# Head norms of a hybrid decoder step: squares summed in two column groups, inverse roots from exp and ln

## The chip, the cores and the metric

The kernel runs on one core of a Trainium2 chip. The metric is the device time in microseconds of one execution. The core's engines work side by side, each through its own queue in order: TensorE (PE), VectorE (DVE), ScalarE (ACT), GpSimd (POOL) and SyncE (SP); DMAs are issued from SP's, ACT's and POOL's queues. Engines wait for each other through semaphores.

## The reference, cut to what matters

One inference step of a one-layer decoder on 512 prompt tokens and 8 x 4 sample tokens, 544 tokens in all. Two branches (retention, and gated linear attention, GLA) have four heads each. The output of each head is normalised over its 128 channels, multiplied by a gain and by a gate, and projected; both branches are mixed by sigmoid gates, and a gated ConvFFN follows.

```python
def group_rmsnorm(o, g):
    B, L, H, dv = o.shape
    of = o.astype(jnp.float32)
    y = of * lax.rsqrt(jnp.mean(of * of, axis=-1, keepdims=True) + EPS)
    y = y.reshape(B, L, H * dv) * g.astype(jnp.float32)
    return y.astype(o.dtype)
...
    y_r = (group_rmsnorm(o_r, g_ret) * jax.nn.silu(rg)) @ w_ret_out
...
    y_g = (group_rmsnorm(o_g, g_gla) * jax.nn.silu(gg)) @ w_gla_out
    mix = jax.nn.sigmoid(m_r) * y_r + jax.nn.sigmoid(m_g) * y_g
    h = x + mix @ w_o
```

The model-wide norms (`rmsnorm` with ln1, ln2, and the last one) have the same form over 1024 channels.

## The kernel before, in words

Activations lie transposed: channels on the 128 partitions, the 544 tokens along the free axis, in two halves of 272 (`HALF`), since a PSUM bank takes one half. All large products are made of three single-pass products of a high and a low part of weights and activations (`whi`, `wlo`, `nhi`, `nlo`): ACT copies a weight block from `raw` to `whi`, DVE subtracts to get `wlo`, and SP loads the next block when `wlo` is done.

The stage of the change is the middle of the program. `middle_order()` writes one list of steps, and each engine walks through that list and issues its own part of every step. The order of every queue is thus written by hand. The list goes through 15 units of 256 columns of the input projection (PE: `product`, line 2050; two halves j of 128 columns), and puts the small steps of the branches between them. Steps that matter here, for head h: `gsq`/`rsq` (ACT squares the head's output into `gsq`), `gn`/`rn` (PE sums the squares over the partitions by a matmul with ones; ACT takes the square root), `gi`/`ri` (DVE inverts the root and scales the head), `sl` (ACT's silu of the gate, tile `ysil`), `y1` (DVE: head times gate), `y2` (ACT makes the high part `yhi`, DVE the low part `ylo`), `rk`, `rs`, `rp`, `ro`, `rx`, `rw` (the retention of one head: keys, masked scores, states, output, sample states). g is GLA, r is retention. The eight norms come in the order gn0, gn1, gn2, gn3, rn0, rn1, rn2, rn3.

The small products share PSUM tile `ax`, two banks at a time in turn: PE takes banks (`aux_take`) when the use two before is drained, sets `aux_filled`, and the engine that reads them sets `aux_drained`. The roots go to `grs` and `grs1` in turn, so norm n waits until DVE has scaled norm n-2 (`o_ready`). There is one `gsq` for the head norms: a square waits until PE has summed the one before.

The parts of a head norm, one line for each engine:

```python
run(gsq[:, :], normed(NORMS[n]), ACT.Square, osq_done)                      # ACT, L1160
small(bank(name, a)[:, 0:HALF], ones, sq[:, HALF * a:HALF * (a + 1)], ...)  # PE, L2089
run(halves(grs2[norms % 2][:, :]), bank2(s), ACT.Sqrt, drained_sem(s), scale=1.0 / DV, bias=eps)  # ACT, L1165
inverse(root[:, :], s, dve_step)                                            # DVE, L1648
dve.scalar_tensor_tensor(normed(s), normed(s), vec(...), root[:, :], ...)   # DVE, L1653
```

After the list come the gate units (`GATES`): PE computes the sigmoid gates of the two branches in two units of two halves each, and DVE drains each half from PSUM into `gsig` (line 1465, `scaled`). A second gate unit's half j begins on PE when the first unit's half j is drained:

```python
for j in range(2):
    pe.wait_ge(drained[j], F0[j] + g)
    product(j, u % 2, j, every, nhi, nlo).then_inc(filled[j], 1)
```

DVE reaches that first drain after the last steps of the list, which are `ri` 3, `y2` 5, `y1` 6, `y1` 7, `y2` 6, `y2` 7. POOL begins there to add weight blocks in DRAM by accumulating DMAs (`v_weight_sum`).

Of the kernel before, what the change touches and what calls it, by code (L numbers as in the profile page):

```python
# [31 lines left out]
P = 128  # L32
# [5 lines left out]
HALF = NT // 2  # L38
# [171 lines left out]
def build(nc, A, O):  # L210
# [7 lines left out]
    def at(name, shape, off, dt=F32):  # L218
        return nc.alloc_sbuf_tensor_at(name, shape, dt, offset=base + off)
# [85 lines left out]
    gsq, grs = at("gsq", [P, NT], o), at("grs", [P, NT], o + T)  # L305
    hsq = [sqt, gsq]
    grs2 = [grs, at("grs1", [P, NT], C + 11 * T)]
    o += 2 * T
# [85 lines left out]
    def halves(t):  # L394
        return t.rearrange("p (a b) -> p a b", a=2)

    def bank(name, b):
        return ax[:, 2 * (USE[name] % 2) + b, :]

    def bank2(name):  # L400
        k = 2 * (USE[name] % 2)
        return ax[:, k:k + 2, 0:HALF]

    def sem(name):
        return ctx.enter_context(nc.semaphore(name))
# [26 lines left out]
    sq_done, acc_done = sem("sq_done"), sem("acc_done")  # L432
    rstd_ready = sem("rstd_ready")

# [183 lines left out]
    def aux_wait_filled(eng, name):  # L618
        k = USE[name]
        eng.wait_ge(aux_filled[k % 2], k // 2 + 1)  # L620

    def aux_wait_drained(eng, name):
        k = USE[name]
        eng.wait_ge(aux_drained[k % 2], k // 2 + 1)
# [7 lines left out]
    def filled_sem(name):  # L632
        return aux_filled[USE[name] % 2]

    def drained_sem(name):
        return aux_drained[USE[name] % 2]
# [386 lines left out]
    def _(act):  # L1023
        st = Steps(act, act_step)

        def run(out, in_, func, done, **kw):
            return act.activation(out, in_, func, **kw).then_inc(done, 1)  # L1027
# [22 lines left out]

        def root(name, width):

            aux_wait_filled(act, name)
            run(halves(rstd[:, :]), bank2(name), ACT.Sqrt, drained_sem(name), scale=1.0 / width, bias=eps)

# [7 lines left out]
        for s in ORDER:  # L1063
# [35 lines left out]
            elif k == "rstd1":  # L1099
                root("rstd1", D_MODEL)  # L1100
            elif k == "v":
# [59 lines left out]
            elif k in ("gn", "rn"):  # L1161
                aux_wait_filled(act, s)
                if norms > 1:
                    act.wait_ge(o_ready, norms - 1)
                run(halves(grs2[norms % 2][:, :]), bank2(s), ACT.Sqrt, drained_sem(s), scale=1.0 / DV, bias=eps)  # L1165
                norms += 1
# [127 lines left out]
        for n in range(4):  # L1294
# [9 lines left out]
            hi(u + 2, u % 2, 32 * (u // 2 + 2), (filled[1], FW[1] + n + 1))  # L1304
        root("rstd2", D_MODEL)

# [142 lines left out]
    def _(dve):  # L1449
# [16 lines left out]

        def inverse(out, name, done):
            aux_wait_drained(dve, name)
            dve.reciprocal(out, out).then_inc(done, 1)  # L1469

        adds = [0]
# [24 lines left out]
        for s in ORDER:  # L1496
# [35 lines left out]
            elif k == "rstd1":  # L1532
                inverse(rstd[:, :], "rstd1", rstd_ready)
                dve.wait_ge(rstd_ready, 1)
# [110 lines left out]
            elif k in ("gi", "ri"):  # L1645
                s = ("gn" if k == "gi" else "rn", s[1])
                root = grs2[norms % 2]
                inverse(root[:, :], s, dve_step)  # L1648
                st.n += 1
                st.wait()  # L1650
                h = s[1]
# [180 lines left out]
        for n in range(4):  # L1832
# [12 lines left out]
            lo(u + 2, u % 2, u + 3)  # L1845
        inverse(rstd[:, :], "rstd2", rstd_ready)
        dve.memset(ext[:, 0:2], 0.0).then_inc(conv_done, 1)
# [191 lines left out]
    def _(pe):  # L2039
# [45 lines left out]
        def summed(name, sq):  # L2085

            aux_take(pe, name)
            for a in range(2):
                small(bank(name, a)[:, 0:HALF], ones, sq[:, HALF * a:HALF * (a + 1)],  # L2089
                      done=filled_sem(name) if a else None)  # L2090
# [73 lines left out]
        for s in ORDER:  # L2164
# [132 lines left out]
            elif k in ("gn", "rn"):  # L2297
                pe.wait_ge(osq_done, NORMS.index(s) + 1)
                summed(s, gsq)
            elif k == "rk":  # L2300
# [269 lines left out]
```

## Time and profile before

| what | value |
|---|---|
| median of 3 runs | 824.47 us (824.27 to 825.74) |
| the profiled execution: its own time | 826.43 us |
| its span | 824.6 us |
| granted TensorE clock, mean | 0.997 of full speed |
| PE, DVE, ACT, POOL busy | 815.2, 587.9, 376.4, 217.0 us |
| the stage of the head norms | about 158 to 266 us |
| busy in 155 to 262: PE, DVE, ACT, POOL | 106.15, 88.90, 44.24, 46.29 of 107 us |
| busy in 220 to 262: PE, DVE, ACT, POOL | 41.15, 39.35, 19.48, 17.26 of 42 us |

Matmuls are pipelined: the time that one holds PE is read from start to next start, not from its length. A bracket at the end of a row says how long the engine was idle before it, and who ended that.

### The profile page before, as it was taken

Reading aid. Unit: us, or ns where it says so; the run is one execution under the profiler, and the core shown is the slowest. Engines: PE = TensorE matmul, PEld = TensorE weight load, DVE = VectorE, ACT = ScalarE, POOL = GpSimd, SP = SyncE. Lnnn points to the kernel's source line nnn. Section 1 sums busy time; section 2 is a strip of 40 time slices with the busy share of each in tenths; the row PEclk is TensorE's granted clock in tenths of the full one; section 3 lists DMA queues with packets and bytes.
Section 4 is the critical chain, followed back from the end, with each engine's and each line's share of the span. In section 5 each row is a group of like instructions: output and inputs, shape, how many; then the busy total and the mean of one; then the engine's idle time right before and its main releaser. Section 6 shows DMA issues by size and latency. Waiting matters only on the chain.

```text
span 824.6 us, 15722 instructions
## 1 busy us (share of the span) xinstructions
PE 815.2 (99%) x6528; PEld 801.7 (97%) x6528; DVE 587.9 (71%) x765; ACT 376.4 (46%) x528; POOL 217.0 (26%) x258
## 2 busy tenths in 40 slices
PE   9999999999999999999999999999999999999996
PEld 9999999999989999999999999999999999999996
DVE  4465768487899877766558877777777756778973
ACT  5554234332456363543344544444444424544574
POOL 4018246443427400000530333333222322000020
PEclk9999999999999999999999999999999999999998
DMA  8769978983327973547996687576677874765622
GB/s 270 220 204 152 252 228 189 204 248 115 127 77 137 213 243 115 179 137 234 189 275 199 124 261 217 142 203 191 246 190 204 230 171 102 200 181 172 174 63 108
DMA packets 163025, 152.29 MB, mean 185 GB/s; under 512 B 6677, under 2 KB 144617, under 8 KB 162940
## 3 DMA queue, kind: packets, MB, share of 16 engines
q1 hardware_dynamic: 129420, 109.73, 42.8%
q0 software_dynamic: 33376, 41.05, 26.6%
q8 instruction: 50, 0.82, 0.4%
q10 hardware_dynamic: 160, 0.53, 0.2%
q14 instruction: 19, 0.16, 0.1%
HBM read 145.32 MB, written 58.40 MB: 247 GB/s over the span
## 4 chain that ended last, share of the span: by engine, by line
PE 96%; DVE 3%; issue 0%; ACT 0%; DVEq 0%
PE mm L2050 52%; PE ax L2356 14%; PE mm L2470 8%; PE ax L2470 6%; PE ax L2069 6%; PE mm L2356 4%; PE ax L2074 3%; PE mm L2131 1%; PE mm L2069 1%; DVE grs L1469 1%; PE mm L2062 0%; DVE ysil L1712 0%; DVE ylo L1717 0%; DVE wlo L1729 0%; DVE wlo L1459 0%
## 5 line engine op out<-in xcount | busy, mean ns | idle before, releaser
L2050 PE MATMUL mm<-nhi,whi 128*128 128x272 f32 x928 | 196.2, 293 | 0.0
L2050 PE MATMUL mm<-nhi,wlo 128*128 128x272 f32 x928 | 191.9, 288 | 0.0
L2050 PE MATMUL mm<-nlo,whi 128*128 128x272 f32 x928 | 191.4, 288 | 0.0
L1027 ACT ACTIVATE whi<-raw 128x1024 fp32r<-128x1024 f32 (+3 forms) x112 | 128.5, 1181 | 64.8 <-PE mm L2050 34.7
L2050 PEld LDWEIGHTS mm<-nhi,whi 128*128 128x128 f32 x928 | 146.2, 188 | 2.9 <-issue 1.1
L2050 PEld LDWEIGHTS mm<-nlo,whi 128*128 128x128 f32 x928 | 145.8, 188 | 0.0
L2050 PEld LDWEIGHTS mm<-nhi,wlo 128*128 128x128 f32 x928 | 145.0, 189 | 0.0
L1729 DVE TENSOR_TENSOR wlo<-raw,whi 128x1024 fp32r<-128x1024 f32 (+1 forms) x78 | 84.4, 1123 | 5.9 <-ACT whi L1027 3.5
L1459 DVE TENSOR_TENSOR wlo<-raw,whi 128x2048 fp32r<-128x2048 f32 x27 | 65.2, 2414 | 14.7 <-ACT whi L1027 14.6
L958 POOL DMA_DIRECT2D v_sums<-in_w_up x24 | 30.7, 4230 | 117.4 <-DVE mlo L1800 115.8
L1027 ACT ACTIVATE whi<-ring 128x1408 fp32r<-128x1408 f32 x25 | 34.6, 1383 | 44.1 <-PE ax L2470 24.0
L2470 PE MATMUL mm<-bhi,whi 128*128 128x272 f32 x176 | 51.4, 292 | 0.0
L1961 DVE TENSOR_TENSOR wlo<-ring,whi 128x1408 fp32r<-128x1408 f32 x25 | 40.6, 1624 | 14.6 <-ACT whi L1027 14.6
L2470 PE MATMUL mm<-bhi,wlo 128*128 128x272 f32 x176 | 50.7, 288 | 0.0
L2470 PE MATMUL mm<-blo,whi 128*128 128x272 f32 x176 | 50.5, 287 | 0.0
L992 POOL TENSOR_TENSOR gl<-gl,rstd 128x544 f32<-128x544 f32 x22 | 39.5, 1797 | 27.8 <-ACT gl L1027 27.8
L2356 PE MATMUL ax<-nhi,whi 128*128 128x272 f32 x144 | 41.5, 288 | 0.0
L2356 PE MATMUL ax<-nhi,wlo 128*128 128x272 f32 x144 | 41.4, 288 | 0.0
L2356 PE MATMUL ax<-nlo,whi 128*128 128x272 f32 x144 | 41.4, 288 | 0.0
L1027 ACT ACTIVATE cb<-ext,vecs 128x560 f32<-128x560 f32 x22 | 18.7, 852 | 48.5 <-DVE ext L1867 48.5
L1873 DVE SCALAR_TENSOR_TENSOR cb<-ext,vecs,cb 128x560 f32<-128x560 f32 x22 | 19.1, 870 | 28.4 <-ACT cb L1027 28.4
L1027 ACT ACTIVATE bhi<-gact 128x1088 fp32r<-128x1088 f32 (+2 forms) x29 | 23.1, 796 | 35.2 <-DVE gact L1900 31.0
(393 smaller groups left out, 1979.4 us busy)
## 6 DMA issues: line engine op xcount, KB each, us to landing
raw<-in_w_in SPq DMA_DIRECT2D x36, 512.0 KB, 5.2
raw<-in_w_up SPq DMA_DIRECT2D x36, 512.0 KB, 7.0
ring<-w_sums SPq DMA_DIRECT2D x16, 704.0 KB, 4.9
w_sums<-in_w_down SPq DMA_DIRECT2D x9, 768.0 KB, 10.5
w_sums<-in_w_down POOLq DMA_DIRECT2D x9, 768.0 KB, 9.5
ring<-in_w_down SPq DMA_DIRECT2D x9, 704.0 KB, 4.6
v_sums<-in_w_up SPq DMA_DIRECT2D x24, 256.0 KB, 7.8
v_sums<-in_w_up POOLq DMA_DIRECT2D x24, 256.0 KB, 14.7
```

The costliest lines, as they stand in the source:

```text
L958: pool.dma_start(v_sum(n, i), added(i), accum_op=ALU.add).then_inc(vs_done[n], 16)
L992: pool.tensor_tensor(gl[j][:, :], gl[j][:, :], rstd[:, :], ALU.mult).then_inc(gl_scaled, 1)
L1027: return act.activation(out, in_, func, **kw).then_inc(done, 1)
L1459: dve.tensor_tensor(wlo[s][:, :, :], raw[s][:, :, :], whi[s][:, :, :].bitcast(F32), ALU.subtract).then_inc(lo_ready, 1)
L1729: dve.tensor_tensor(flat(wlo[s])[:, c], flat(raw[s])[:, c], flat(whi[s])[:, c].bitcast(F32), ALU.subtract).then_inc(lo_ready if i else glo ...
L1873: st.did(dve.scalar_tensor_tensor(cb[:, 0:CONV], ext[:, 1:1 + CONV], vec(V_CW + KF + t), cb[:, 0:CONV], op0=ALU.mult, op1=ALU.add))
L1961: dve.tensor_tensor(dlo[s][:, :, :], w[:, :, :], dhi[s][:, :, :].bitcast(F32), ALU.subtract).then_inc(lo_ready, 1)
L2050: ins = pe.matmul(mm[:, 2 * j + a, 0:HALF], w, x[:, kx, HALF * a:HALF * (a + 1)], start=first and n == 0 and m == 0, stop=last and n == le ...
L2069: ins = pe.matmul(out, w, x, start=start, stop=stop, skip_group_check=True)
L2074: ins = pe.transpose(out, in_, ident[0:in_.shape[0], 0:in_.shape[0]])
L2356: ins = pe.matmul(out, w, x, start=start and k == 0 and m == 0, stop=k == 3 and m == 2, skip_group_check=True)
L2470: ins = pe.matmul(b, w, x, start=k == 0 and n == 0 and p != 3, stop=k == KH - 1 and n == 2, skip_group_check=True)
```

## The change

The eight head norms: PE sums the squares with 64 columns of ones instead of 128, the first half of the tokens into partitions 0 to 63 of one bank and the second half into partitions 64 to 127 of the same bank. Each partition then holds one half's sums. ACT takes the logarithm of all 128 partitions (272 columns) into a tile `logs`, and then exp(-0.5 x), which is the inverse root, for each half of the partitions into its half of the tokens in `grs`. Two DMAs on ACT's queue, 64 partitions x 272 columns each, carry each half to the other 64 partitions. DVE no longer inverts; it waits for both DMAs (`root_in`) and scales.

The two model-wide roots `rstd1` and `rstd2` keep their full-width sums; ACT makes them by ln and exp too, and DVE's reciprocal goes. The last norm is as before.

```diff
+    logs = [at(f"logs{k}", [P, HALF], C + o4) for k, o4 in enumerate((8 * T, 10 * T + 2 * DV * 4))]
...
-        def root(name, width):
+        def inverse_root(name, width):
             aux_wait_filled(act, name)
-            run(halves(rstd[:, :]), bank2(name), ACT.Sqrt, drained_sem(name), scale=1.0 / width, bias=eps)
+            run(halves(rstd[:, :]), bank2(name), ACT.Ln, drained_sem(name), scale=1.0 / width, bias=eps)
+            aux_wait_drained(act, name)
+            run(rstd[:, :], rstd[:, :], ACT.Exp, rstd_ready, scale=-0.5)
...
             elif k in ("gn", "rn"):
                 aux_wait_filled(act, s)
+                i = norms % 2
+                log, root = logs[k == "rn"], grs2[i]
+                run(log[:, :], bank(s, 0)[:, 0:HALF], ACT.Ln, drained_sem(s), scale=1.0 / DV, bias=eps)
+                aux_wait_drained(act, s)
                 if norms > 1:
                     act.wait_ge(o_ready, norms - 1)
-                run(halves(grs2[norms % 2][:, :]), bank2(s), ACT.Sqrt, drained_sem(s), scale=1.0 / DV, bias=eps)
+                for r, t in zip(PAIR, HALVES):
+                    run(root[r, t], log[r, :], ACT.Exp, root_ready, scale=-0.5)
+                act.wait_ge(root_ready, 2 * (norms + 1))
+                for a in range(2):
+                    act.dma_start(root[PAIR[1 - a], HALVES[a]], root[PAIR[a], HALVES[a]]).then_inc(root_in[i], 16)
                 norms += 1
...
-        def inverse(out, name, done):
-            aux_wait_drained(dve, name)
-            dve.reciprocal(out, out).then_inc(done, 1)
...
             elif k in ("gi", "ri"):
-                inverse(root[:, :], s, dve_step)
-                st.n += 1
-                st.wait()
+                dve.wait_ge(root_in[norms % 2], 32 * (norms // 2 + 1))
...
             elif k in ("gn", "rn"):
                 pe.wait_ge(osq_done, NORMS.index(s) + 1)
-                summed(s, gsq)
+                aux_take(pe, s)
+                for r, t in zip(PAIR, HALVES):
+                    small(bank(s, 0)[r, 0:HALF], ones[:, 0:GLA_DK], gsq[:, t], done=filled_sem(s) if r is PAIR[1] else None)
```

PE's queue keeps its order; the two matmuls of each norm are 64 columns wide. On ACT, the queue at the last norm, rn3, before (`grs` is the root, `whi` the split of the weights of the unit after the list, `ysil` the silu pair 6 and 7, `yhi` the high parts):

```order
L1027 ACTIVATE gsq<-qk 128x544 [waits aux_filled1,aux_drained0]
L1027 ACTIVATE yhi<-ysil_190 128x544 [waits y_prod]
L1027 ACTIVATE whi_51<-raw_49 128x2048 [waits filled1,landed0]
L1027 ACTIVATE grs_123<-ax,c_66 128x544 [waits o_ready,aux_filled0]
L1027 ACT_TABLE_LOAD
L1027 ACTIVATE ysil_192<-ysil_192 128x544 [waits drained0]
L1027 ACTIVATE ysil_193<-ysil_193 128x544 [waits drained1]
L1027 ACTIVATE yhi<-ysil_191 128x544 [waits y_prod]
```

and now (`logs` is the logarithm; two rows `ysil` and the following `yhi` are as before):

```order
L1030 ACTIVATE whi_51<-raw_49 128x2048 [waits filled1,landed0]
L1030 ACT_TABLE_LOAD
L1030 ACTIVATE logs_124<-ax,c_66 128x272 [waits aux_filled0]
L1030 ACT_TABLE_LOAD [waits o_ready]
L1030 ACTIVATE grs_125<-logs_124 64x272 [waits aux_drained0]
L1030 ACTIVATE grs_125<-logs_124 64x272
L1178 DMA grs_125<-grs_125 64x272 [waits root_ready]
L1178 DMA grs_125<-grs_125 64x272
L1030 ACT_TABLE_LOAD
L1030 ACTIVATE ysil_194<-ysil_194 128x544 [waits drained0]
```

Where one row stood between the weights and the silu pair's table load, eight stand now, two of them table loads. The other norms have the same seven rows (and the load of the logarithm's table) in place of their `grs` row.

On DVE, at the norms rn0 and rn1 before (`qk` is the scaled head, `ysil2` a product with a gate, `ysil5` the drain of a projection half, `wlo1` the low weights):

```order
L1469 RECIPROCAL grs_122<-grs_122 128x544 [waits aux_drained0]
L1653 SCALAR_TENSOR_TENSOR qk_70<-qk_70,vecs_67,grs_122 128x544 [waits dve_step]
L1712 TENSOR_TENSOR ysil2_188<-ysil2_188,gqk_71 128x544 [waits o_ready,silu_done]
L1469 RECIPROCAL grs1_123<-grs1_123 128x544 [waits aux_drained1]
L1653 SCALAR_TENSOR_TENSOR qk_70<-qk_70,vecs_67,grs1_123 128x544 [waits dve_step]
L1717 TENSOR_TENSOR ylo_78<-ysil0_186,yhi_77 128x544 [waits y_hi]
L1465 TENSOR_TENSOR ysil5_191<-mm,rstd_68 128x544 [waits filled1,y_prod]
L1459 TENSOR_TENSOR wlo1_54<-raw1_50,whi1_52 128x2048 [waits hi_ready]
```

and now:

```order
L1659 SCALAR_TENSOR_TENSOR qk<-qk,vecs,grs 128x544 [waits root_in0]
L1718 TENSOR_TENSOR ysil_190<-ysil_190,gqk 128x544 [waits o_ready,silu_done]
L1659 SCALAR_TENSOR_TENSOR qk<-qk,vecs,grs_125 128x544 [waits root_in1]
L1723 TENSOR_TENSOR ylo<-ysil_188,yhi 128x544 [waits y_hi]
L1478 TENSOR_TENSOR ysil_193<-mm,rstd 128x544 [waits filled1,y_prod]
L1472 TENSOR_TENSOR wlo_54<-raw_50,whi_52 128x2048 [waits hi_ready]
```

The reciprocals are gone; the scaling itself waits for the DMAs, and the rows behind it keep their order.

## Rows read from the trace of the kernel before

**Rows 1.** The page, part 1: busy us (share of the span) xinstructions.

```profile
PE 815.2 (99%) x6528; PEld 801.7 (97%) x6528; DVE 587.9 (71%) x765; ACT 376.4 (46%) x528; POOL 217.0 (26%) x258
```

**Rows 2.** The chain that ended last, in time: start us, us, what.

```profile
254.72 30.13 PE mm L2050 x240
...
444.83 30.82 PE mm L2050 x246
```

**Rows 3.** Timeline of PE, sample states (185) and gn2 (195): start, us, instruction.

```profile
185.17 0.41 PE L2050 MATMUL mm<-nhi,wlo 128*128 128x272 f32 x2
185.52 0.64 PE L2069 MATMUL ax<-s0r,rqs 128*32 128x256 f32 x8
186.09 1.16 PE L2069 MATMUL ax<-rsc,vr 128*128 128x128 f32 x8
...
195.20 1.08 PE L2069 MATMUL ax<-gsq,c 128*128 128x272 f32 x4
196.12 0.71 PE L2074 MATMUL ax<-c,qk 128*128 128x128 f32 x5
...
199.67 1.08 PE L2069 MATMUL ax<-gsq,c 128*128 128x272 f32 x4
```

**Rows 4.** Timeline of ACT at gn2: the root, and the square behind it.

```profile
196.32 0.71 ACT L1027 ACTIVATE grs<-ax,c 128x544 f32<-128x544 f32 x1 [3.50 <-PE ax L2069]
196.93 0.65 ACT L1027 ACTIVATE gsq<-gqk 128x544 f32<-128x544 f32 x1
```

**Rows 5.** Groups by form, ACT: xcount, busy us, mean ns, idle before.

```profile
L1027 ACT ACTIVATE osq<-resid 128x272 f32<-128x272 f32 x16 | 6.3, 416 | 5.0 <-DVE resid L1953 5.0
```

**Rows 6.** One line's instructions, a DMA issue on ACT: ns min/median/max.

```profile
L1444 ACTq DMA_DIRECT2D out<-y_nat x1: 385/385/385, 819.4 to 819.4; - x1
```

**Rows 7.** Timeline of ACT behind rn3.

```profile
253.90 1.92 ACT L1027 ACTIVATE whi<-raw 128x2048 fp32r<-128x2048 f32 x1 [0.20 <-PE mm L2050]
...
256.43 1.28 ACT L1027 ACT_TABLE_LOAD   x1
257.72 1.21 ACT L1027 ACTIVATE ysil<-ysil 128x544 f32<-128x544 f32 x2
258.83 0.64 ACT L1027 ACTIVATE yhi<-ysil 128x544 fp32r<-128x544 f32 x1
```

**Rows 8.** The tile grs, DVE's reciprocals: ns min/median/max, first and last start.

```profile
L1469 DVE RECIPROCAL grs<-grs x8: 3529/3546/3553, 172.9 to 258.1; 128x544 f32<-128x544 f32 x8
```

**Rows 9.** DMA issues: xcount, KB each, median us from issue to landing.

```profile
out<-y_nat ACTq DMA_DIRECT2D x1, 512.0 KB, 4.6
...
out<-rst POOLq DMA_DIRECT2D x4, 64.0 KB, 3.5
...
raw<-in_w_in SPq DMA_DIRECT2D x2, 32.0 KB, 2.3
```

**Rows 10.** Timeline of PE: rn1, rn2, rn3, first matmuls of gate unit 2.

```profile
225.16 1.08 PE L2069 MATMUL ax<-gsq,c 128*128 128x272 f32 x4
...
245.84 1.16 PE L2069 MATMUL ax<-gsq,c 128*128 128x272 f32 x4 [0.71 <-DVE rss L1683]
...
253.64 1.08 PE L2069 MATMUL ax<-gsq,c 128*128 128x272 f32 x4
...
266.58 0.48 PE L2050 MATMUL mm<-nhi,whi 128*128 128x272 f32 x2
```

**Rows 11.** Timeline of DVE, from rn1's scaling to the first gate drain.

```profile
232.02 0.79 DVE L1653 SCALAR_TENSOR_TENSOR qk<-qk,vecs,grs 128x544 f32<-128x544 f32 x1
...
245.53 0.17 DVE L1683 TENSOR_TENSOR rss<-ax,c 32x32 f32<-32x32 f32 x1
...
261.64 0.79 DVE L1653 SCALAR_TENSOR_TENSOR qk<-qk,vecs,grs 128x544 f32<-128x544 f32 x1
262.34 0.72 DVE L1717 TENSOR_TENSOR ylo<-ysil,yhi 128x544 fp32r<-128x544 f32 x1
...
265.70 0.72 DVE L1465 TENSOR_TENSOR gsig<-mm,rstd 128x544 f32<-128x544 f32 x1
```

More of the change, by code:

```diff
@@ L306, in build @@
     hsq = [sqt, gsq]
+    logs = [at(f"logs{k}", [P, HALF], C + o4) for k, o4 in enumerate((8 * T, 10 * T + 2 * DV * 4))]
+    assert 2 * DV * 4 + HALF * 4 <= T
     grs2 = [grs, at("grs1", [P, NT], C + 11 * T)]
@@ L432, in build @@
     sq_done, acc_done = sem("sq_done"), sem("acc_done")
-    rstd_ready = sem("rstd_ready")
+    rstd_ready, root_ready = sem("rstd_ready"), sem("root_ready")
+    root_in = [sem(f"root_in{i}") for i in range(2)]
     last_sq, last_sums, last_roots, last_rstd = map(sem, ("last_sq", "last_sums", "last_roots", "last_rstd"))
@@ L1099, in _ @@
             elif k == "rstd1":
-                root("rstd1", D_MODEL)
+                inverse_root("rstd1", D_MODEL)
             elif k == "v":
@@ L1304, in _ @@
             hi(u + 2, u % 2, 32 * (u // 2 + 2), (filled[1], FW[1] + n + 1))
-        root("rstd2", D_MODEL)
+        inverse_root("rstd2", D_MODEL)
         for i in range(KF // 2):
@@ L1532, in _ @@
             elif k == "rstd1":
-                inverse(rstd[:, :], "rstd1", rstd_ready)
                 dve.wait_ge(rstd_ready, 1)
@@ L1845, in _ @@
             lo(u + 2, u % 2, u + 3)
-        inverse(rstd[:, :], "rstd2", rstd_ready)
+        aux_wait_drained(dve, "rstd2")
         dve.memset(ext[:, 0:2], 0.0).then_inc(conv_done, 1)
```

## The prediction

> **What bounds the kernel now.** I read the busy times first. TensorE (PE) is busy for 99% of the 824.6 us span, VectorE (DVE) for 71%, ScalarE (ACT) for 46% [rows 1]. So the end moves only by what PE's queue gains or waits. Next the chain of waits: from 254.72 PE runs 240 matmuls in 30.13 us, which is 0.1255 us each with nothing between them, and so again from 444.83 [rows 2]. The change touches ten roots. Two of them (the model-wide norms) lie off PE's path: behind the second one PE runs from 444.83 for 30.82 us without a pause, and the first has the same shape; there the shorter root only gives DVE slack, and I cost it at nothing. The eight head norms lie between 164 and 262 us. There I read PE, ACT and DVE side by side in the timeline and asked at each norm what PE waits for afterwards. Three places came out: norm gn3 (PE waits for a square on ACT), norm rn2 (PE waits for DVE), and the start of the second gate unit (PE waits for a drain that DVE does last after all norms).
>
> The sum is made against the profiled span. That execution took 826.43 us; the median of the plain runs is 824.47, and I put the difference onto the median.
>
> **PE's part.** A norm's two matmuls hold PE for 0.92 us (195.20 to 196.12) [rows 3]: four passes of 0.23. After the change the two write different 64-column halves of the array. The nearest row is the sample-state product, four matmuls on 32-column groups: PE's pair before it starts at 185.17 and lasts 0.25, so 185.42, and the next full matmul starts at 186.09, so it holds PE for 0.67. Its eight passes of 256 columns one after another would take 8 x 0.217 = 1.73; side by side the two passes of each group take 0.43, so 0.24 is a fixed cost. For the norm that gives 0.46 + 0.24 = 0.70, a gain of 0.22 each. Bounds: 0.46 (no fixed cost) and 0 (no overlap). I take 0.22, from the row of the same kind.
>
> The Trainium skill's "TensorEngine Tiling (Array Packing)" (Overview, Key Properties) gives up to 2x for two column groups, and says that a change of tiling mode drains the engine. The first alone would be the 0.46 bound, 1.2 us less than my sum; the 0.24 in the row goes with the second.
>
> **ACT's part, per norm.** Now: one Sqrt of 0.71 [rows 4]. After: a logarithm on 272 columns, between 0.42 (a 272-column pass) [rows 5] and 0.71 (the full-width root with the same bias operand), I take 0.50; a table load, 1.28; two exponentials of 0.42 that overlap a little, 0.75; two DMA issues on ACT's own queue, 0.385 each by ACT's one such row [rows 6], 0.77; gaps 0.10. The load before the logarithm can go while ACT waits, except where ACT is late. The loads are not a guess: the built program has one before each of the two functions. A load costs 1.28 and no more: the table row at 256.43 ends at 257.71 and the next pass starts at 257.72 [rows 7].
>
> The Trainium skill's "ScalarE: Activation LUTs" (What ACT_TABLE_LOAD costs) speaks against the change: it counts a drain of about 1.38 us on top of each load. The trace doesn't agree, with 0.01 us behind the load here. By that figure my sum would be about 7 us worse.
>
> **DVE's part.** Eight reciprocals of 3.55 go, 28 us [rows 8]; in their place stands a wait for two DMAs. Their landing has no row of its own kind (partition to partition). Nearest: 2.3 for 32 KB on SP's queue, 3.5 for 64 KB on GpSimd's queue, 4.6 for 512 KB on ACT's queue [rows 9]. Each new one is 68 KB. I take 2.3, counted from the issue's start, because 32 KB is the nearest row of a hardware queue; below 2.3 I see no row of such a queue, above it 4.6.
>
> **First place, gn2 to gn3.** The square for gn3 stands on ACT behind gn2's root. Now the Sqrt starts 1.12 after the matmuls (195.20 to 196.32), the square follows, and PE takes gn3 at 199.67, 4.47 after gn2 began, without waiting. After: logarithm at 0.70 + 0.20 = 0.90, then 0.50 + 1.28 + 0.75 + 0.77 + 0.65 (square) + 0.10 = 4.05, so 4.95. PE would be there at 4.25: a new wait of 0.70, and gn3 starts 0.48 later, counted from gn2, than now. The other squares have us of slack.
>
> **Second place, rn1 to rn2.** rn1 starts at 225.16 now; in the sum four gains and that 0.48 put it 0.40 earlier. DVE scales with its root at 232.02, 6.86 later [rows 10, 11]. After: second issue starts 0.90 + 0.50 + 1.28 + 0.75 + 0.385 + 0.10 = 3.92 behind rn1, lands at 6.22: 0.64 sooner, so DVE is 1.04 earlier there, in spite of 28 us less work, and has stood idle for some 5 us. What is queued behind that wait on DVE is the whole row up to the mask product that ends at 245.70, for which PE waits 0.71 at rn2 (245.84). So rn2 moves by -1.04, while PE alone could have come 0.71 + 0.40 + 0.22 = 1.33 earlier.
>
> **Third place, rn3 to the second gate unit.** rn3 thus starts 1.26 earlier. Now PE begins gate unit 2 at 266.58, 12.94 after rn3 (253.64) [rows 10], and just then: the drain that it needs starts at 265.70 and takes 0.72 [rows 11]. DVE does it after rn3's scaling, the last products and their low parts. Here ACT is not idle beforehand, so every load counts. From rn3's start: weight split to 2.18 [rows 7], load to 3.48, logarithm to 3.98, load to 5.28, exponentials to 6.04, issues to 6.87, load for the sigmoid-linear pair to 8.17, the pair 1.11, to 9.28, the high part yhi to 9.92. DVE's low part can start at 10.0; from that row to PE's start are 4.24 now (262.34 to 266.58), so 14.24. By the landing: 6.48 + 2.3 = 8.8, plus 4.94 (261.64 to 266.58), is 13.75, so ACT's chain decides, and a landing up to 2.8 is free here. PE comes to the gate unit 14.24 after rn3 and not 12.94: +1.30.
>
> Sum: -1.26 + 1.30 = +0.04. From there on PE has its own pace again. **Forecast: no change, 824.5 us.** The gain on PE is made and given back at the gate unit. With the bounds of the column groups (five of the gains count): 823.3 to 825.6.
>
> **Rivals.**
> 1. Slower: the landings take 3.5, as for 64 KB. Then rn2's side loses 1.2 and the end of the norms 0.7 more: 824.5 + 1.9 = 826.4; with 4.6 it is 2.3 + 1.8, 828.6. It costs from 2.3 up at rn1 and from 2.8 up at rn3. For it: at rn3 GpSimd's weight sums begin to fill the DMA engines. Against it: little is in flight at rn1. Chance 0.20.
> 2. Faster: DVE, rid of 28 us, runs ahead, and nothing on ACT or in the DMAs holds PE. Then PE keeps eight gains and the wait at rn2: 8 x 0.22 + 0.71 = 2.5, so 822.0. For it: DVE is what PE waits for at rn2 and, within 0.2 us, at the gate unit. Against it: the three sums above. Chance 0.12.
> 3. The column groups don't run side by side (the change doesn't do what it says): five times 0.22 are lost, 825.6, still no change by my bound. Against it: the 0.67 row. Chance 0.05.
> 4. Slower: a switch of tables costs ACT twice its load. One more load's time at gn3, one at rn1, three at the end: 5 x 1.28 = 6.4, so 830.9. Against it: the 0.01 us behind the load. Chance 0.02. This is the case that "ScalarE: Activation LUTs" would have, in the Trainium skill.
> The forecast keeps 0.61.
>
> **How the numbers follow.** A measurement of this kernel can tell about 0.2%, 1.65 us, from no change: 822.8 to 826.1. The forecast and rival 3 lie inside (0.66), rivals 1 and 4 above (0.22), rival 2 below (0.12). The range 822.4 to 827.0 takes in the column bounds and landings up to some 3.8, and leaves out most of rival 2, the far part of rival 1 and rival 4.
>
> **What would show it.** In the profile after: PE's gsq matmuls about 0.70 from start to next start; a table load and two DMA issues in each norm on ACT; PE waiting some 0.7 at gn3; DVE idle some 5 us before rn1's and rn3's scaling, released by a DMA; PE late at the first matmul of gate unit 2 by over 1 us, released by DVE's gsig drain. It is wrong if PE runs through the gate unit without a pause (rival 2), or if DVE's waits end 3 us or more after the issues (rival 1).

## The result, and the profile after

The changed kernel takes 833.91 us (median; 832.34 to 834.38), the kernel before 824.47: the ratio is 1.0099, with a 95% interval of 1.0088 to 1.011. So it is slower by about 8 us. Forecast was no change, 824.5, in a range of 822.4 to 827.0; the range does not hold the time. The page of the changed kernel, busy times and the granted clock in 40 slices (to compare with [rows 1]):

```profile
PE 815.9 (98%) x6528; PEld 799.5 (96%) x6528; DVE 552.1 (66%) x755; ACT 401.1 (48%) x560; POOL 217.1 (26%) x258
...
PEclk9999999999999899999999999999999999999998
```

DVE has 36 us less to do, ACT 25 us more, and PE as much as before in a span that is 8.0 us longer (832.6). One slice of the clock, from about 271 to 291 us, reads 8 where the kernel before has 9 (the last slice reads 8 in both). The timeline of PE says where the time went (start, us, instruction; in brackets the wait and who ended it). The rows answer to [rows 3] and [rows 10]: gn2, gn3, rn1, one transpose, rn2, the sample states behind it, rn3, and the first two matmuls of gate unit 2.

```profile
195.31 0.68 PE L2075 MATMUL ax<-gsq,c 128*64 128x272 f32 x4
...
200.70 0.68 PE L2075 MATMUL ax<-gsq,c 128*64 128x272 f32 x4 [1.01 <-ACT gsq L1030]
...
225.97 0.68 PE L2075 MATMUL ax<-gsq,c 128*64 128x272 f32 x4
...
237.70 0.74 PE L2080 MATMUL ax<-c,qk 128*128 128x128 f32 x5 [0.34 <-ACT qk L1030]
...
245.80 0.68 PE L2075 MATMUL ax<-gsq,c 128*64 128x272 f32 x4
246.92 0.64 PE L2075 MATMUL ax<-s0r,rqs 128*32 128x256 f32 x8 [0.44 <-issue]
...
253.84 0.68 PE L2075 MATMUL ax<-gsq,c 128*64 128x272 f32 x4
...
272.88 0.79 PE L2056 MATMUL mm<-nhi,whi 128*128 128x272 f32 x2 [6.14 <-DVE gsig L1478]
273.46 0.66 PE L2056 MATMUL mm<-nlo,whi 128*128 128x272 f32 x2
```

Up to rn3 the two kernels keep step: 253.64 before, 253.84 now. Gate unit 2 then starts 19.04 us after rn3 instead of 12.94. PE stands for 6.14 us, and DVE's drain ends that wait. DVE itself waited (scaling of rn1, rn2, rn3, the weights' low part ahead of the last, and the drain; see [rows 11]):

```profile
231.98 0.78 DVE L1659 SCALAR_TENSOR_TENSOR qk<-qk,vecs,grs 128x544 f32<-128x544 f32 x1 [3.91 <-DMA grs<-grs]
...
251.84 0.79 DVE L1659 SCALAR_TENSOR_TENSOR qk<-qk,vecs,grs 128x544 f32<-128x544 f32 x1 [5.02 <-DMA grs<-grs]
...
255.95 2.29 DVE L1472 TENSOR_TENSOR wlo<-raw,whi 128x2048 fp32r<-128x2048 f32 x1 [0.29 <-ACT whi L1030]
267.95 0.78 DVE L1659 SCALAR_TENSOR_TENSOR qk<-qk,vecs,grs 128x544 f32<-128x544 f32 x1 [9.71 <-DMA grs<-grs]
...
272.01 1.35 DVE L1478 TENSOR_TENSOR gsig<-mm,rstd 128x544 f32<-128x544 f32 x2
```

Before, DVE had rn3's root inverted by 261.6 and scaled at 261.64; now it is idle for 9.71 us and scales at 267.95. ACT is not what it waits for. ACT's timeline behind rn3 (see [rows 7]; between `whi` and the silu pair's load stand seven rows now where one stood), and the piece of the chain of waits from its two issues to DVE:

```profile
254.00 1.92 ACT L1030 ACTIVATE whi<-raw 128x2048 fp32r<-128x2048 f32 x1 [0.20 <-PE mm L2056]
255.94 1.28 ACT L1030 ACT_TABLE_LOAD   x1
257.23 0.49 ACT L1030 ACTIVATE logs<-ax,c 128x272 f32<-128x272 f32 x1
257.74 1.28 ACT L1030 ACT_TABLE_LOAD   x1
259.03 0.88 ACT L1030 ACTIVATE grs<-logs 64x272 f32<-64x272 f32 x2
259.95 1.80 ACTq L1178 DMA_DIRECT2D grs<-grs  x2
261.78 1.28 ACT L1030 ACT_TABLE_LOAD   x1 [1.86 <-issue]
263.08 1.21 ACT L1030 ACTIVATE ysil<-ysil 128x544 f32<-128x544 f32 x2
264.19 0.64 ACT L1030 ACTIVATE yhi<-ysil 128x544 fp32r<-128x544 f32 x1
```

```profile
259.95 0.47 ACTq L1178
...
260.45 7.48 DMA grs<-grs
```

ACT begins to issue the second copy at 260.45. The copy of 68 KB lands 7.48 us later. At rn1 the same copy took 2.07 (second issue at 229.91, DVE at 231.98). Over all sixteen the trace gives 1.9, 4.0 and 7.5 as least, median and most; the second copies of gn2, gn3 and rn0 took 3.9 to 4.2. The stretches in which rn1's and rn3's copies were under way, and five stretches at gate unit 2 (us of the stretch, busy of PE, PEld, DVE, ACT, POOL, then PE's clock, the DMA engines' share as the profile counts it, which can exceed 1, and GB/s):

```profile
229.90:232.00 2.10, 2.10 (x22) 1.69 (x19) 0.02 (x1) 1.35 (x2) 0.00 (x0) 1.00 0.29 66
...
260.40:268.00 7.60, 6.34 (x51) 6.12 (x49) 0.04 (x1) 3.04 (x4) 7.60 (x11) 1.00 1.20 242
...
268.00:270.00 2.00, 0.00 (x0) 0.00 (x0) 2.00 (x4) 0.00 (x0) 2.00 (x5) 1.00 1.45 181
270.00:272.00 2.00, 0.00 (x0) 0.00 (x0) 1.91 (x4) 1.96 (x4) 2.00 (x4) 0.50 1.44 180
272.00:274.00 2.00, 1.12 (x5) 1.15 (x6) 1.97 (x5) 1.98 (x4) 2.00 (x2) 0.50 1.45 181
...
276.00:278.00 2.00, 2.00 (x15) 2.00 (x15) 1.97 (x4) 1.30 (x2) 2.00 (x3) 0.80 1.45 181
278.00:280.00 2.00, 2.00 (x19) 2.00 (x18) 1.36 (x1) 0.00 (x0) 0.59 (x1) 1.00 1.44 180
```

Two things are to be seen. While rn3's copies are under way 242 GB/s are moved in all; rn1's had the DMA engines nearly to themselves, since two copies of 68 KB in 2.1 us are themselves about 66 GB/s. And the granted clock of PE is still 1.00 from 268 to 270, falls to 0.50 (1.2 GHz, the lower of its two levels) at about 270, while PE still stands, and stays there for some 4 us after PE has started: the pairs of matmuls behind 273.46 start 0.455 us apart instead of 0.25. The clock is at 1.00 again by 278.

**A marker.** Profiled executions differ by up to 2.5 us in when the stage begins at all (gn0 starts between 161.80 and 164.34), so below I count within an execution: from gn0 to rn3, from rn3 to gate unit 2, and from rn3 to ACT's start on the second model-wide root (444.87 before, 452.94 now), behind which PE has no further wait in either kernel. Before: 89.53, 12.94 and 191.23. Now: 89.50, 19.04 and 199.10. So from rn3 to the marker 7.87 us are lost: 6.10 up to gate unit 2, and 1.77 behind it.

### The profile page after: what moved, and what is told of

Its sections match the earlier page's. It is cut to its first block, busy times and chain, and to the rows that moved or that the text cites. A ratio compares the mean times of both kernels' runs of the same rounds, so it can differ in the third digit from the quotient of the medians.

```text
span 832.6 us, 15760 instructions
## 1 busy us (share of the span) xinstructions
PE 815.9 (98%) x6528; PEld 799.5 (96%) x6528; DVE 552.1 (66%) x755; ACT 401.1 (48%) x560; POOL 217.1 (26%) x258
## 4 chain that ended last, share of the span: by engine, by line
PE 93%; ACT 3%; DVE 1%; issue 1%; DMA 1%; ACTq 0%; DVEq 0%
PE mm L2056 51%; PE ax L2364 14%; PE mm L2478 8%; PE ax L2478 6%; PE ax L2075 6%; PE mm L2364 4%; PE ax L2080 2%; PE mm L2137 1%; PE mm L2075 1%; ACT L1030 1%; DMA grs<-grs 1%; PE mm L2068 0%; ACTq L1178 0%; ACT grs L1030 0%; ACT whi L1030 0%
## 5 line engine op out<-in xcount | busy, mean ns | idle before, releaser
L1472 DVE TENSOR_TENSOR wlo<-raw,whi 128x2048 fp32r<-128x2048 f32 x27 | 63.2, 2339 | 20.6 <-ACT whi L1030 20.5
L2478 PE MATMUL ax<-bhi,whi 128*128 128x272 f32 x132 | 38.1, 288 | 0.0
```

Of the source, the lines that this page charges most:

```text
L1472: dve.tensor_tensor(wlo[s][:, :, :], raw[s][:, :, :], whi[s][:, :, :].bitcast(F32), ALU.subtract).then_inc(lo_ready, 1)
L2478: ins = pe.matmul(b, w, x, start=k == 0 and n == 0 and p != 3, stop=k == KH - 1 and n == 2, skip_group_check=True)
```

## The experiments

My theory after the result: the copies of rn3 land late because of the transfers beside them, PE waits for that, and its clock falls; all else of the change costs almost nothing. The rivals: copies and issues cost something at every norm; ACT's queue is slow with such copies as such; the table loads are what delays DVE; the clock fell for a reason of its own. All results in one table (times in us; ratio to the kernel before with its 95% interval, each against runs of the kernel before on the same chip, whose median lay between 824.47 and 825.97; "landing" is that of rn3's second copy; "rest" is what is lost from rn3 to the marker beyond the later start of the gate unit):

| kernel | median | ratio | gn0 to rn3 | rn3 to gate 2 | rn3 to marker | landing | rest |
|---|---|---|---|---|---|---|---|
| before | 824.47 | | 89.53 | 12.94 | 191.23 | | |
| after | 833.91 | 1.0099 (1.0088 to 1.011) | 89.50 | 19.04 | 199.10 | 7.48 | 1.77 |
| e1_rn3_old | 825.79 | 1.0004 (0.9994 to 1.0014) | 89.39 | 12.94 | 191.24 | | 0.01 |
| e2_pool_hold | 833.00 | 1.0102 (1.0086 to 1.0119) | 89.49 | 16.37 | 197.74 | 4.81 | 3.08 |
| e3_pool_sp_hold | 829.63 | one run | 89.53 | 14.57 | 196.57 | 2.06 | 3.71 |
| e10_sp_hold | 831.24 | one run | 89.50 | 17.49 | 198.47 | 5.93 | 2.69 |
| e4_direct | 826.24 | 1.001 (1.0 to 1.0021) | 88.53 | 14.32 | 192.61 | none | 0.00 |
| e5_full | 824.29 | 0.9982 (0.9973 to 0.9992) | 88.19 | 13.50 | 191.80 | none | 0.01 |
| e7_roots_only | 825.54 | 0.9996 (0.9987 to 1.0005) | 89.52 | 12.94 | 191.22 | none | -0.01 |
| e6_best | 823.37 | 0.997 (0.9959 to 0.9981) | 87.65 | 12.94 | 191.25 | none | 0.02 |
| e8_busy | 836.67 | 1.0124 (1.0109 to 1.014) | 89.48 | 23.37 | 201.69 | 7.7 | 0.03 |
| e9_busy24 | 836.16 | 1.0132 (1.0095 to 1.0169) | 89.52 | 19.35 | 197.72 | 7.88 | 0.08 |
| e11_after | 834.52 | 1.0109 (1.0093 to 1.0124) | 89.78 | 19.73 | 199.30 | 8.16 | 1.28 |
| e12_busy20 | 837.77 | 1.0129 (1.0102 to 1.0156) | 89.50 | 19.67 | 199.41 | 8.20 | 1.45 |

**e1_rn3_old: the last norm alone in the old form.** In PE's, ACT's and DVE's part of the step, for `s == ("rn", 3)` only:

```diff
+                if s == ("rn", 3):
+                    run(halves(grs2[norms % 2][:, :]), bank2(s), ACT.Sqrt, drained_sem(s), scale=1.0 / DV, bias=eps)
...
+                if s == ("rn", 3):
+                    aux_wait_drained(dve, s)
+                    dve.reciprocal(root[:, :], root[:, :]).then_inc(dve_step, 1)
...
+                if s == ("rn", 3):
+                    summed(s, gsq)
```

> Only the last norm, rn3, goes back to the old form (two full-width sums, square root, DVE's reciprocal, no copies); the other seven norms stay as changed. Theory (all of the loss comes from the late landing of rn3's two copies, 7.5 us, and the clock that fell behind PE's wait of 6.14 us): PE starts gate unit 2 within 0.5 us of 266.58 as in the kernel before, the clock stays up, time 824.3 (823.5 to 825.2). Rival (the copies and issues cost something at every norm): more than half of the 8 us stay, time over 828.

The whole loss is gone: 12.94 from rn3 to gate unit 2, 191.24 to the marker, and no difference from before in the time. Seven changed norms together cost and gain nothing (89.39 against 89.53), and the eighth costs the 8 us. PE's rows at rn3 and at the gate unit, where there is no wait:

```profile
251.46 1.08 PE L2087 MATMUL ax<-gsq,c 128*128 128x272 f32 x4
...
264.40 0.47 PE L2068 MATMUL mm<-nhi,whi 128*128 128x272 f32 x2
```

**e2, e3 and e10: what stands beside rn3's copies.** Two sources move data there: GpSimd's accumulating weight sums, and SyncE's load for a later unit (two transfers of 256 and 768 KB, 1.0 MB in all, issued at 258.3 and 258.8; the expectations put it at 1.25 MB). Each is held, in e2 and e10, and both in e3, until DVE has scaled with rn3's root:

```diff
+        pool.wait_ge(o_ready, 8)
         v_weight_sum(G_3, all_sums, lambda i: v_block(0, 1, i))
...
             sp.wait_ge(lo_ready, u - 1)
+            if u == U_BLOCK:
+                sp.wait_ge(o_ready, 8)
```

> The changed kernel, but GpSimd begins its accumulating weight sums only after DVE has scaled with rn3's root; nothing else moves. Theory (rn3's copies wait for DMA engines that the weight sums fill): landing 2 to 4 us instead of 7.5; then ACT's chain decides (silu pair's table at 261.8, high part done by 264.9, plus 4.24): PE starts gate unit 2 at 268.5 to 269.1 instead of 272.88; time 826.5, or 827.8 if the clock falls there too. Rival (the landing is a matter of ACT's queue or of copies as such, not of the traffic): landing stays at 7 or more, time 833.

> As the run before, and SyncE's load of 1.25 MB that is issued at 258.3 to 259.3 is held as well until DVE has scaled with rn3's root, so that nothing is in flight beside rn3's two copies. Theory (traffic): landing 2.1 us, as at rn1 and rn2, where the DMA engines were 0.1 busy; PE's start of gate unit 2 is then ACT's, 268.5 to 269.1, as in the run before. If the load was the main cause and not the weight sums, the landing drops only here. The later load may cost some us further on; the landing is what is looked at. Rival (queue or copies as such): 7 or more still.

> Only SyncE's load of 1.25 MB is held until DVE has scaled with rn3's root; GpSimd's weight sums run as in the changed kernel. With both held the landing was 2.06 us, with the sums alone held 4.8, with neither 7.5. If the two sources add, the landing is here 2.1 + (7.5 - 4.8) = 4.8; if the sums are the main cause and the load adds only beside them, 6 or more; if the load is all of it, 2 to 2.5 and the second source of the 7.5 is something else. PE's wait at gate unit 2 follows the landing; the later load may hold PE once more further on.

The chain of waits from the second issue on, in e2 and in e10 (start, us, what), and the stretches in which the copies were under way, in e2, e10 and e3 (columns as above):

```profile
258.74 4.81 DMA grs<-grs
```

```profile
257.91 5.93 DMA grs<-grs
```

```profile
258.70:263.60 4.90, 4.90 (x41) 4.90 (x40) 0.03 (x1) 3.04 (x4) 0.00 (x0) 1.00 0.69 202
```

```profile
257.90:263.90 6.00, 6.00 (x50) 6.00 (x49) 0.04 (x1) 3.04 (x4) 6.00 (x11) 1.00 1.33 174
```

```profile
258.30:260.30 2.00, 2.00 (x18) 2.00 (x18) 0.00 (x0) 1.37 (x2) 0.00 (x0) 1.00 0.30 70
```

With nothing beside it the landing is 2.06 (e3: second issue at 258.27, DVE at 260.33), with the load alone 4.81, with the sums alone 5.93, with both 7.48 in the first profile and 7.7 to 8.2 in the four others (e8, e9, e11, e12). The queue and the kind of copy are the same in all. So it is the traffic, and that rival falls. The sums alone bring the larger part. Simple addition would give 2.06 + 2.75 + 3.87, or 8.7, more than any of the five; e2, e3 and e10 are one profile each. How the traffic delays the copies is not shown: from e3 over e2 and e10 to the changed kernel the landing rises, but neither the GB/s (70, 202, 174, 242) nor the engines' share (0.30, 0.69, 1.33, 1.20) rises in step with it.

As for the times, I missed with e2: I expected 826.5 or 827.8 and got 833.0. The landing was 4.81 where I had allowed 4, so PE still waited 3.47, its clock fell to 0.50 there too, and 3.08 us more went by up to the marker, about 0.5 of them in a wait for the low part of weights further on. In e10 PE waited 4.59 at the gate unit and the clock cost 2.69. In e3 the clock stayed up at the gate unit, but PE waited 1.91 for the held load's weights at 303 us, and the clock fell behind that.

**e4_direct: no copies at all.** ACT can read 64 partitions and write the other 64 (the kernel's rotary step does that), so the two copies become two more exponentials:

```diff
                 for r, t in zip(PAIR, HALVES):
-                    run(root[r, t], log[r, :], ACT.Exp, root_ready, scale=-0.5)
-                act.wait_ge(root_ready, 2 * (norms + 1))
-                for a in range(2):
-                    act.dma_start(root[PAIR[1 - a], HALVES[a]], root[PAIR[a], HALVES[a]]).then_inc(root_in[i], 16)
+                    for to in PAIR:
+                        run(root[to, t], log[r, :], ACT.Exp, root_ready, scale=-0.5)
```

> The two copies of each norm go: ACT writes each half of the inverse root itself to both halves of the partitions, four exponentials of 64 partitions instead of two and two issues. The column groups, the logarithm and the table loads stay. Theory (landing): no DMA left; ACT has the root 0.49 + 1.28 + 4 x 0.43 = 3.5 us after the logarithm's start; gn3's wait falls from 1.01 to about 0.6; PE has no wait at rn2; at rn3 ACT's chain with three table loads puts gate unit 2 at about 267.6 to 268.1, 1.0 to 1.5 later than before; time 825.5 (824.8 to 826.5). Rival (table loads and ACT's longer chain are the loss, not the copies): time stays over 829.

As expected, with the time near the upper end. The same three table loads stand behind rn3, and the loss is 1.38 us there, not 7.87. So the table loads are not the loss. That separates the prediction's two paths: ACT's chain is worth 14.32 from rn3 to gate unit 2, the landing is worth 19.04. PE's wait of 1.43 left the clock at 1.00. Up to rn3 the kernel gains 1.00. ACT behind rn3, and PE at the gate unit:

```profile
257.96 1.79 ACT L1030 ACTIVATE grs<-logs 64x272 f32<-64x272 f32 x4
259.76 1.28 ACT L1030 ACT_TABLE_LOAD   x1
261.06 1.21 ACT L1030 ACTIVATE ysil<-ysil 128x544 f32<-128x544 f32 x2
262.17 0.64 ACT L1030 ACTIVATE yhi<-ysil 128x544 fp32r<-128x544 f32 x1
```

```profile
267.08 0.49 PE L2054 MATMUL mm<-nhi,whi 128*128 128x272 f32 x2 [1.43 <-DVE gsig L1476]
```

**e5_full: logarithm and exponential without column groups and copies.**

```diff
+                run(halves(root[:, :]), bank2(s), ACT.Ln, drained_sem(s), scale=1.0 / DV, bias=eps)
+                aux_wait_drained(act, s)
+                run(root[:, :], root[:, :], ACT.Exp, root_ready, scale=-0.5)
...
+                summed(s, gsq)
```

> The column groups and the copies go, the logarithm and the exponential stay: each head norm has its two full-width sums as before, ACT takes a logarithm of 544 columns and one exponential of 544 columns in place, DVE takes no reciprocal. Theory (the landing and PE's wait behind it are the loss, the functions are not): PE holds each sum as long as before, gn3 has no wait, DVE is early and PE's wait of 0.71 at rn2 is gone; at rn3 ACT's chain is 0.9 shorter than with four half exponentials (14.32 from rn3 to the gate unit there), so 13.4 against 12.94 before: PE waits about 0.5. Sum -0.2: time 824.4 (823.8 to 825.2), no change. Rival (two table loads per norm on ACT are a loss of their own): over 826.

The rival falls: the functions on ACT are a small gain, 0.18%, and not a loss. I was right on the gate unit (13.50 against 13.4) and too low on the way to rn3: 1.34 us are gained there instead of 0.71, since a second wait of PE, 0.28 us ahead of the transposes at 240.45 before, goes as well as that at rn2.

```profile
252.28 1.08 PE L2071 MATMUL ax<-gsq,c 128*128 128x272 f32 x4
...
265.78 0.49 PE L2052 MATMUL mm<-nhi,whi 128*128 128x272 f32 x2 [0.40 <-DVE gsig L1474]
```

**e7_roots_only: the two model-wide roots alone.** The head norms are as before; the diff is that of e1 without its condition.

> Only the two model-wide roots use the logarithm and the exponential; all eight head norms are as in the kernel before (full-width sums, square root, reciprocal). Prediction and theory: these two lie off PE's path and cost or gain nothing: 824.6, within 0.1% of before, and PE has the same waits as before (0.71 at rn2, none at the gate unit). Rival: two more table loads late in the program hold PE at the second of them: over 825.5.

The prediction had costed these two at nothing. They cost nothing: 191.22 to the marker, 0.73 for PE's wait at rn2 as before, and a time within its interval of before.

**e8, e9 and e12: the clock.** Small matmuls fill PE's wait at gate unit 2 in the changed kernel, 48, 24 and 20 of them:

```diff
+                    if g == 1 and j == 0:
+                        for _ in range(24):
+                            small(bank(("rn", 3), 1)[:, 0:P], ones, ident)
                     pe.wait_ge(drained[j], F0[j] + g)
```

> The changed kernel with 48 additional small matmuls (128 columns, about 0.12 us each, 5.7 us, into a bank that nobody reads) on PE just ahead of its wait at gate unit 2; they compute nothing that is used. Theory (the granted clock fell because PE stood idle for 6.14 us): PE's queue waits under 1 us there, the granted clock stays at 1.0, the first gate matmul starts no earlier than before, 19.0 us after rn3, and the 1.7 us that the lower clock cost are back: time 832.2. Rival (the clock fell for another reason, such as the load of the other engines and the DMAs at that place): the clock falls all the same, 833.9.

> As the run with 48 additional matmuls, which took 0.22 us each instead of 0.12 and held PE 4.2 us longer than the wait; now 24 of them, 5.3 us, so that they end before DVE's drain. They compute nothing that is used. Theory (the clock fell because PE stood idle for 6.14 us): the gate unit starts 19.0 us after rn3 as in the changed kernel, PE's queue is idle for under 1 us, the granted clock stays at 1.0, and from rn3 to the end it takes 577.0 us instead of 578.8; time about 832.2. Rival (the clock fell for another reason): 578.8 and a clock of 0.5 behind the wait.

> The changed kernel with 20 additional matmuls (4.4 us by 0.22 each) ahead of PE's wait at gate unit 2; they compute nothing that is used. Up to the second model-wide root the run with 24 had won back the clock's loss (197.7 us from rn3 to that root instead of 199.1), but its whole time was 836, with a wait of 3.0 us for a late load of weights at 660 us. If that late load was a chance of those runs: the whole time is now 1.5 to 1.8 us below its partner's, about 831.5. If the added matmuls or the shifted stage bring it about each time: over 834 and the wait at 660 us is there again.

The partner of e12 on its chip was the changed kernel itself, with 834.52 a little over what was expected, and a clock of 0.50:

> The changed kernel itself, unaltered, as the partner on the same chip for the run with 20 additional matmuls: 832 to 834, 1.0% slower than before; clock 0.5 behind PE's wait at gate unit 2.

In e8 I had taken 0.12 us for such a matmul from the page's transposes; they took 0.22, and overran the wait. In e9 they fit (its row counts two passes for each matmul). PE and the stretch behind the start of the gate unit in e9, and the stretch at the same place in e8:

```profile
264.88 5.52 PE L2075 MATMUL ax<-c 128*128 128x128 f32 x48
271.50 0.52 PE L2056 MATMUL mm<-nhi,whi 128*128 128x272 f32 x2 [1.10 <-DVE gsig L1478]
...
272.00:274.00 2.00, 2.00 (x18) 2.00 (x17) 1.93 (x6) 1.99 (x3) 0.54 (x1) 1.00 1.45 181
```

```profile
272.00:274.00 2.00, 2.00 (x20) 2.00 (x19) 1.97 (x5) 1.98 (x4) 2.00 (x2) 1.00 1.45 180
```

DVE, ACT and the DMA engines are as busy there as in the changed kernel in 272 to 274 (1.45 of the DMA share), and the clock stays at 1.00; PE idle is what differs. In e9 the gate unit starts 6.41 later than before and the marker is 6.49 later: the rest is 0.08 instead of 1.77. So the 1.77 are the clock's. In e12 PE still waited 2.30 behind its 20 matmuls, the clock fell, and the rest was 1.45.

The whole times of e9 and e12 don't show that gain; there I was wrong twice. Both profiles have a new wait of PE at 661 and 665 us (3.0 and 3.1 us), with a clock of 0.50 behind it, for a load of 1 MB, of which the second half of 512 KB took 13.85 and 13.98 us to land; the profile of the unaltered kernel beside e12 has none, and one of e12's five runs, at 832.08, was below all of its partner's. In e12 that load was issued at 648.59, in the changed kernel's first profile at 648.40, beside the same work. Why it is late is open, and that it is late in the other slow runs of these two kernels is a guess from their times.

**e6_best: what the runs point to.** e4's form for seven norms, the old form for rn3, and the square for gn3 ahead of gn2's root on ACT:

```diff
-4: [("gn", 2), ("rk", 1), ("gsq", 3), ("gi", 2)]
+4: [("gsq", 3), ("gn", 2), ("rk", 1), ("gi", 2)]
```

> A version from what the runs before showed: the first seven norms as changed but with four exponentials written straight to both halves instead of two and two copies, the square for gn3 put ahead of gn2's root on ACT, and the last norm, rn3, in the old form with root and reciprocal. Theory: up to rn3 PE gains 1.0 (as the run without copies showed) and gn3's wait of 0.67, and from rn3 on it runs as in the kernel before: rn3 1.0 to 1.7 us earlier, no wait at gate unit 2, time 823.0 (822.5 to 824.0), 0.1 to 0.2% faster than before. If DVE's chain at the gate unit does not follow PE's earlier start, PE gives the gain back there: 824.3.

As expected, with 823.37 for 823.0. PE has no wait at gn3, none at rn2 and none at the gate unit; rn3 comes 1.88 us earlier and the rest is as before. It is faster than both kernels, by 0.3% against the one before.

```profile
250.67 1.08 PE L2087 MATMUL ax<-gsq,c 128*128 128x272 f32 x4
...
263.61 0.47 PE L2068 MATMUL mm<-nhi,whi 128*128 128x272 f32 x2
```

## Why the prediction was wrong, step by step

**The step that failed** is "a landing up to 2.8 is free here" at the third place, with the 2.3 that it was held against. The path through the landing was right in all its other parts. The prediction had 6.48 to the second issue, the landing, and 4.94 from DVE's scaling to PE. Measured: 6.61 (253.84 to 260.45), 7.48, 0.02, and 4.93 (267.95 to 272.88), together 19.04. With 2.3 for 7.48 ACT's chain decides, with 7.48 the copies do. The forecast of ACT's chain, 14.24, was measured apart in e4 as 14.32 and in e3 as 14.57. In the changed kernel itself it would be about 15.3 (the high part `yhi` ends 10.99 after rn3, where 9.92 was forecast), since the two issues held ACT for 1.80 there; so the landing still decided, but with issues that long a landing of 2.3 would also have missed the forecast, by about 1.

**Why the landing was mis-sized.** I chose the row by size and queue: 32 KB on SyncE's queue, 2.3 [rows 9]. That is what a copy takes with nothing beside it (2.06 to 2.07 at rn1 and in e3), and at the first seven norms, some of which took twice that, being wrong cost nothing. At rn3 the place decided and not the size: GpSimd's sums and SyncE's load were under way. Rival 1 named that ("at rn3 GpSimd's weight sums begin to fill the DMA engines") and still priced it by rows of larger copies elsewhere, 3.5 and 4.6. The upper bound should have come from what the same stretch held: of what was issued from 250 to 262 us, the trace before gives 12.4 us to landing (median) for the sums themselves, and 6.8 and 8.8 for SyncE's two transfers. ("Above it 4.6" also overlooked rows: 132 and 128 KB on SyncE's queue landed in 2.3 and 2.4. They would have spoken for 2.3 all the more; size was not the matter.) With 7.48 in rival 1's own formula (2.8 free) the gate unit comes out 4.7 later than in the forecast; measured are 4.80 (19.04 for 14.24).

The Trainium skill's "DMA: Bandwidth & Descriptors" (Queues, rings and completion order) says that the queues don't have DMA engines of their own, and that each engine serves them in turn, a packet at a time. The runs agree so far: ACT's queue held nothing but the two copies, and they took 2.06 alone and 7.48 beside what the other queues moved. The turns themselves no run shows.

**The clock** is a term that the sum did not have. PE's wait of 6.14 at the gate unit was followed by a granted clock of 0.50, and 1.77 us went there (e9). Rivals 1 and 4 had waits of several us and no such term either.

**The sum, by its terms,** from gn0 to the marker. Forecast: rn3 1.26 earlier and the gate unit 1.30 later in its turn, +0.04. Measured: rn3 0.03 earlier, the gate unit 6.10 later, the clock 1.77: 7.84. The difference is 1.23 + 4.80 + 1.77.

**The 1.23 that PE did not gain up to rn3.** Three terms: 0.67 + 0.31 + 0.25.

- *The column groups, 0.67.* 0.22 per norm was forecast, 1.10 for the five up to rn1; PE got 0.43. The sums themselves are shorter by 0.31 from start to next start (0.61, [rows 3] has 0.92), but the work around them starts later. From the full product ahead of the sums to the one behind, rn3 has 2.31 (253.00 to 255.31) where it had 2.42, and gn0, rn0 and rn1 show about the same 0.11; gn2 shows 0.16. At gn1 nothing is left, since PE then waits 0.28 for DVE (`rks`). The sample-state row had hidden what it costs to go in and out. So rival 3 (no overlap) is wrong, and half of the gain is there.
- *gn2 to gn3, 0.31.* A wait of 0.70 was forecast; it was 1.01. The logarithm was right (0.49 for 0.50), the exponentials took 0.88 for 0.75, and the two issues 1.12 for 0.77: ACT's one issue in the trace before [rows 6] was too cheap a row.
- *From rn1 to rn3, 0.25.* PE was to gain 0.86 there and gained 0.61. The wait of 0.71 at rn2 went, and with it another of 0.28 ahead of it; but PE now waits 0.34 at the transpose of 237.70, where ACT copies `qk` behind rn1's root, and 0.44 at the sample states behind rn2. The sum had looked only at the squares and at rn2.

**The second place** was right in kind only. The root of rn1 was there 6.01 after rn1 (6.22 forecast), and PE's wait at rn2 went. But rn1 came 0.81 later (0.23 of that is the later start of the whole stage) and not 0.40 earlier, so DVE scaled at the same time as before (231.98 for 232.02), and rn2 stood at 245.80 for 245.84. The sample states behind it began at 246.92, for 246.96 before. The trace names no releaser for those 0.44, but by the order of the banks they take those that DVE's last row of that stretch (`rst`) drains by 246.82: PE's wait for DVE had mostly moved on by one step.

**Rival 4** stays down: the logarithm starts 0.01 behind the load that ends at 257.22, the exponential 0.01 behind the next. The model-wide roots cost nothing (e7), as forecast. And the signs in the profile that the prediction named as proof against it came: DVE's wait at rn3 ended over 3 us after the issues.

## What to carry to other kernels

Price a transfer that is put on the path by what else is under way at its place, and take the bound from the transfers of that stretch, however small the new one is: a copy of 68 KB took 2.06 us alone and 7.5 to 8.2 beside two other sources. When work leaves an engine with 28 us of it and comes back as a wait, ask first whether the last instance of the wait is followed by the engine that bounds the kernel; seven of eight were harmless here. Where an engine can write the data to its place itself, as ACT does in e4, that was the cheaper way here: e4 takes 1.001 of the time before where the copies took 1.0099. A gain came with full-width sums (0.18%, e5), and with e4's form for seven norms, the last norm in its old form and a square moved ahead (0.3%, e6).

## What the runs showed of the hardware

- A wait of PE costs more than its length when the granted clock falls behind it. It fell to 0.50 (1.2 GHz) in or behind waits of 2.30, 3.47, 4.59, 6.14 and 6.83 us at the gate unit, and behind one of 1.91 in e3; it stayed at 1.00 (2.4 GHz) behind 0.40, 1.10, 1.43 and 1.68. What it cost did not grow with the wait: 1.77 behind 6.14, 1.28 behind 6.83, 2.69 behind 4.59. The windows say why: PE ran at 0.50 for about 3.9, 2.8 and 6.0 us after these three waits, and the cost is a little under half of that. In the longer waits more of the low stretch passed while PE stood.
- The issue of two copies held ACT for 1.12 us at most norms. At rn3 it was 1.28 to 1.80 in the five profiles with the sums and the load beside them, and 1.12 or 1.13 with one of the two or none (e2, e10, e3).
- ACT moved a half of 64 partitions to the other 64 at the price of an ordinary pass (four take 1.79, two in place 0.88).
